# Two blocks of a transformer on one core: wider first accumulators, an unpaced GpSimd, and the pooling branch moved in among the attention's items

## The reference

```python
def adaln(cond, w, b):                       # w is 1024 x 9*1024
    m = jax.nn.silu(cond) @ w + b
    return m.reshape(m.shape[:-1] + (N_MOD, D_MODEL))

def ffn_sublayer(h, m, g, w13, w2, base):
    hn = modulate(rms_norm(h, g), m[:, :, base], m[:, :, base + 1])
    return h + 0.5 * m[:, :, base + 2] * swiglu_2(hn, w13, w2)

def multiscale_pool(u, pool_w, pool_scale):  # 4 groups of 128 channels, windows 2, 4, 8, 16
    ...
        mean = (jnp.take(cs, hi, axis=1) - jnp.take(cs, lo, axis=1)) / cnt
        outs.append((mean - xg).astype(u.dtype) @ pool_w[g])
    return jnp.concatenate(outs, axis=-1) * pool_scale

def even_mixer(hl, hc, w_in, w_out, rpb, pool_w, pool_scale, ctx_out):
    q, k, v, u = jnp.split(hl @ w_in, [NA_WIDTH, 2 * NA_WIDTH, 3 * NA_WIDTH], axis=-1)
    k_c, v_c = jnp.split(hc @ w_in[:, NA_WIDTH:3 * NA_WIDTH], 2, axis=-1)
    ...
    att = neighbourhood_attention(split_heads(q), split_heads(k), split_heads(v), k_c, v_c, rpb)
    pool = multiscale_pool(u, pool_w, pool_scale)
    y_lat = jnp.concatenate([att, pool], axis=-1) @ w_out
```

## Time and profile before

| | us |
|---|---|
| median of three timed runs | 2839.51 (2833.29 to 2842.50) |
| profiled execution | 2831.01 |
| its span | 2829.1 |
| mean granted TensorE clock | 0.943 |
| PE busy | 2634.2 |
| DVE busy | 1600.5 |
| ACT busy | 1173.0 |
| POOL busy | 1329.1 |

### The profile page before, as it was taken

How to read it: one execution, slowest core, us unless ns; L and a number is a source line. 1 busy time by engine, 2 the same in 40 slices (tenths; PEclk the granted TensorE clock), 3 DMA queues, 4 the chain that set the end, 5 groups by cost and what they waited for, 6 DMA issues and landing times.

```text
span 2829.1 us, 32645 instructions
## 1 busy us (share of the span) xinstructions
PE 2634.2 (93%) x11901; PEld 2141.4 (76%) x11901; DVE 1600.5 (57%) x1619; ACT 1173.0 (41%) x1354; POOL 1329.1 (47%) x689
## 2 busy tenths in 40 slices
PE   7997998899899899799989989998999999999998
PEld 6876766788688776678878777786678878878786
DVE  5664445656666634666666655544247666655544
ACT  4444344444443535444444433443134444353443
POOL 5994110399798211049959959700007535600000
PEclk9998999999999999999999989998579999998999
DMA  7663323567566422368767759843027757653553
GB/s 240 224 212 115 105 86 108 172 226 232 173 221 206 144 90 72 113 206 264 238 210 258 248 144 233 266 149 108 1 75 251 234 172 244 228 164 119 171 184 113
DMA packets 312483, 496.06 MB, mean 175 GB/s; under 512 B 14479, under 2 KB 221611, under 8 KB 312267
## 3 DMA queue, kind: packets, MB, share of 16 engines
q1 hardware_dynamic: 289306, 412.48, 44.8%
q0 software_dynamic: 22800, 81.35, 10.0%
q10 hardware_dynamic: 288, 1.05, 0.1%
HBM read 493.77 MB, written 1.05 MB: 175 GB/s over the span
## 4 chain that ended last, share of the span: by engine, by line
PE 60%; POOL 25%; DVE 5%; ACT 4%; DMA 3%; issue 2%; ACTq 0%; DVEq 0%; SPq 0%; POOLq 0%; PEldq 0%
PE ps L745 55%; POOL arena L688 11%; POOL arena L679 9%; POOL arena L689 3%; DMA raw<-in_ffn_w_dram 2%; PE ps L824 2%; POOL arena L663 2%; DVE wlo L433 2%; ACT whi L420 1%; PE ps L831 1%; PE ps L945 1%; PE ps L762 0%; PE ps L916 0%; ACT work L1212 0%; DVE HTlo L1415 0%
## 5 line engine op out<-in xcount | busy, mean ns | idle before, releaser
L433 DVE TENSOR_TENSOR wlo<-raw,whi 128x2048 fp32r<-128x2048 f32 (+5 forms) x405 | 1086.6, 2686 | 529.0 <-ACT whi L420 526.7
L745 PE MATMUL ps<-whi,HThi 128*128 128x512 f32 (+2 forms) x2360 | 957.5, 406 | 60.1 <-ACT arena L1203 20.2
L420 ACT ACTIVATE whi<-raw 128x2048 fp32r<-128x2048 f32 (+4 forms) x405 | 753.1, 1861 | 494.2 <-PE ps L745 412.2
L745 PE MATMUL ps<-wlo,HThi 128*128 128x512 f32 (+2 forms) x2360 | 932.3, 395 | 0.0
L745 PE MATMUL ps<-whi,HTlo 128*128 128x512 f32 (+2 forms) x2360 | 931.2, 395 | 0.0
L745 PEld LDWEIGHTS ps<-whi,HThi 128*128 128x128 f32 x2360 | 453.0, 192 | 162.1 <-issue 26.9
L688 POOL TENSOR_TENSOR arena<-arena 128x1024 f32<-128x1024 f32 (+1 forms) x184 | 541.0, 2940 | 10.8
L745 PEld LDWEIGHTS ps<-wlo,HThi 128*128 128x128 f32 x2360 | 452.0, 192 | 96.9
L745 PEld LDWEIGHTS ps<-whi,HTlo 128*128 128x128 f32 x2360 | 454.0, 192 | 85.7
L679 POOL TENSOR_TENSOR arena<-arena,cond 128x1024 f32<-128x1024 f32 x184 | 422.4, 2302 | 174.3 <-issue 85.5
L663 POOL DMA_DIRECT2D arena<-in_mod_w_dram x144 | 113.6, 789 | 470.6 <-DVEq L353 421.8
(11 more groups left out here) (196 smaller groups left out, 1756.9 us busy)
## 6 DMA issues: line engine op xcount, KB each, us to landing
raw<-in_ffn_w_dram SPq DMA_DIRECT2D x330, 512.0 KB, 4.7
raw<-in_w_ffn_gu_dram SPq DMA_DIRECT2D x176, 512.0 KB, 4.7
arena<-in_mod_w_dram POOLq DMA_DIRECT2D x144, 512.0 KB, 4.4
raw<-in_w_ffn_down_dram SPq DMA_DIRECT2D x88, 512.0 KB, 4.3
raw<-in_w_in_dram SPq DMA_DIRECT2D x40, 1024.0 KB, 5.1
raw<-in_even_w_in_dram SPq DMA_DIRECT2D x12, 1024.0 KB, 5.0
raw<-in_conv_w_in_dram SPq DMA_DIRECT2D x12, 1024.0 KB, 5.2
raw<-in_w_out_dram SPq DMA_DIRECT2D x8, 1024.0 KB, 5.0
```

Source lines behind the costliest of these rows:

```text
L420: i = nc.scalar.activation(whi[0:rows, r, a:b], raw[0:rows, r, a:b], ACT.Copy)
L433: i = nc.vector.tensor_tensor(wlo[0:rows, r, a:b], raw[0:rows, r, a:b], whi[0:rows, r, a:b].bitcast(F32), ALU.subtract)
L745: return nc.tensor.matmul(o, lhsT, rhs, start=first, stop=last)
```

## The change

- The accumulators of FFN 0 are 512 columns wide (`slots[0]`, twelve in `GT` and two in `C`), and POOL leaves out the last addition for them. PE adds both halves with two products per column instead of one.
- POOL's wait for PE's progress ahead of each piece is gone. For FFN 4 and later POOL waits, once per FFN and ahead of its DMAs, for the sums of earlier shares (`mods_summed`).
- The barriers of `near_turn` and `near` are gone; the turnings wait for the groups that they read (`group_read`), once ahead of them and once at the fifth chunk. The context's dense phase hands the copying of its last group on (`later=True`).
- In the pooling branch only the first group's average stays in `near_turn`, behind the turnings; the rest stands beside the items, a step at every other item. Averages use bank 6, maps bank 7; `pooled` and `pool_out` have places of their own.

```diff
-        slots = {**{f: [flat[:, MOD * i:MOD * (i + 1)] for i in range(24)] for f in (0, 1, 3)},
+        slots = {**{f: [flat[:, MOD * i:MOD * (i + 1)] for i in range(24)] for f in (1, 3)},
+                 0: [flat[:, 512 * i:512 * (i + 1)] for i in range(12)] + [C[:, 0, 512 * i:512 * (i + 1)] for i in range(2)],
...
-                phase("dense", after_norm=True,
+                phase("dense", after_norm=True, later=True,
...
-            if n and not phases[n]["kind"] in ("norm", "ffn", "final") and not phases[n].get("after_norm"):
+            if n and not phases[n]["kind"] in ("norm", "ffn", "final", "near_turn", "near") and not phases[n].get("after_norm"):
...
-        pool_out = [work[:, 512 + j * SEQ:512 + (j + 1) * SEQ] for j in range(2)]
+        pooled = [work[:, 3584 + j * SEQ:3584 + (j + 1) * SEQ] for j in range(2)]
+        pool_out = [flat[:, 5120 + j * SEQ:5120 + (j + 1) * SEQ] for j in range(2)]
...
-                    pool.wait_ge(s_used, ph["u0"] + 3 * (10 * i // len(part)) + 2)
...
-                        for n in (4 * MOD, 2 * MOD):
+                        n = 4 * MOD
+                        while n > acc.shape[-1]:
                             link(nc.gpsimd.tensor_tensor(q[:, 0:n], q[:, 0:n], q[:, n:2 * n], ALU.add))
-                        p = nc.gpsimd.tensor_tensor(acc, q[:, 0:MOD], q[:, MOD:2 * MOD], ALU.add)
+                            n //= 2
+                        p = nc.gpsimd.tensor_tensor(acc, q[:, 0:n], q[:, n:2 * n], ALU.add)
...
+                    if ph["f"] >= 4:
+                        pool.wait_ge(sem("mods_summed"), min(ph["f"] - 1, 5))
...
-            def turn(chunks, done, freed):
+            def turn(chunks, done, freed, at_4=lambda: None, behind=lambda: None):
...
+                    if m == 4:
+                        at_4()
...
+                behind()
...
-                    i = mm(o, acc, cc("ones"))
+                    for j, a in enumerate(acc):
+                        i = mm(o, a, cc("ones"), j == 0, j == len(acc) - 1)
...
-                    turn(near_chunks(), "heads_turned", ("heads_read_dve", "heads_read_act"))
-                    pe.wait_ge(sem("pool_in"), 32)
-                    for n_g in range(5):
...
-                    take("pool_split", 2)
+                    def average(g):
+                        for s in range(NB):
+                            i = mm(ps[:, 6, 0:SEQ], PJ[:, s, 1536 + g * P:1536 + (g + 1) * P], poolA[:, g, s, :], s == 0, s == 1)
+                        i.then_inc(sem("pooled"), 1)
+
+                    def first_average():
+                        pe.wait_ge(sem("pool_in"), 32)
+                        average(0)
+
+                    def pool_step(n):
+                        if n % 2 == 0 and n <= 6:
+                            g = n // 2
+                            take("pooled_copied")
+                            if g:
+                                take("pool_scaled")
+                            mm(ps[:, 7, 0:SEQ], poolW[:, g, :], pooled[g % 2]).then_inc(sem("pool_mapped"), 1)
+                            if g < 3:
+                                average(g + 1)
+
+                    take("group_read")
+                    turn(near_chunks(), "heads_turned", ("heads_read_dve", "heads_read_act"), lambda: take("group_read"), first_average)
...
-                    run_items(near_items())
+                    run_items(near_items(), (), pool_step)
```

More of the change, by code:

```diff
@@ L696, in bias_tiles @@
             def bias_tiles(h):
+                if h >= NA_H:
+                    return
                 rpb = t["na_rpb_2"]
-                for b in range(NB if h < NA_H else 0):
+                for b in range(NB):
                     for r in range(2):
@@ L782, in sums_of @@
                 pe.wait_ge(s_made, made)
-                accs = [acc[:, k * P:(k + 1) * P] for _, m, accs in parts for k in range(MOD // P) for acc in accs]
+                accs = [[acc[:, at:at + P] for at in range(k * P, acc.shape[-1], MOD)]
+                        for _, m, accs in parts for k in range(MOD // P) for acc in accs]
                 columns.extend((ps[:, bank, at:at + 1], acc) for at, acc in enumerate(accs))
@@ L810, in _, with run_items @@
             beside = Beside(part)
-            def run_items(items, places=()):
+            def run_items(items, places=(), between=beside.item):
                 N = len(items)
@@ L841, in run_items @@
                         i.then_inc(sem("item_pv"), 1)
-                    beside.item(n)
+                    between(n)
             def gate_rows(ph, half, bank):
@@ L1181, in turn_dst, with exps @@
                 return [(blocks[0].shape[-1], tile[0:blocks[0].shape[-1], m, :]) for m, blocks in enumerate(src)]
-            def exps(items):
+            def exps(items, between=lambda n: beside.item(n)):
                 for n, it in enumerate(items):
@@ L1345, in _, with pool_step @@
                 elif kind == "near":
-                    exps(near_items())
+                    def pool_step(n):
+                        if n % 2 and 3 <= n <= 9:
+                            take("pool_scaled")
+                            A(HThi[:, 4 + (n - 3) // 2, :], pool_out[(n - 3) // 2 % 2], ACT.Copy).then_inc(sem("pool_hi"), 1)
+                    exps(near_items(), pool_step)
                 elif kind == "near_turn":
                     copy_turned(near_chunks(), 1)
-                    for g in range(4):
-                        take("pool_scaled")
-                        A(HThi[:, 4 + g, :], pool_out[g % 2], ACT.Copy).then_inc(sem("pool_hi"), 1)
                 elif kind == "index":
@@ L1421, in _, with run_items @@
             pv_seen = [0]
-            def run_items(items, ys):
+            def run_items(items, ys, between=lambda n: beside.item(n)):
                 N = len(items)
@@ L1761, in _, with pool_step @@
                     copy_turned(near_chunks(), 0)
[L1762 to L1764 removed]
+                    take("pooled")
+                    V.tensor_copy(pooled[0], ps[:, 6, 0:SEQ]).then_inc(sem("pooled_copied"), 1)
+                elif kind == "near":
+                    out4 = work[:, 2048:3072].rearrange("p (b h d) -> p h b d", b=NB, d=HD)
+                    def pool_step(n):
+                        if n % 2 and n <= 5:
+                            g = (n + 1) // 2
                             take("pooled")
[L1766 to L1768 removed]
+                            V.tensor_copy(pooled[g % 2], ps[:, 6, 0:SEQ]).then_inc(sem("pooled_copied"), 1)
+                        if n % 2 and n <= 7:
+                            g = n // 2
                             take("pool_mapped")
[L1770 removed]
+                            V.tensor_scalar(pool_out[g % 2], ps[:, 7, 0:SEQ], vcol("pool_scale", g), None,
                                             ALU.mult).then_inc(sem("pool_scaled"), 1)
[L1772 to L1773 removed]
+                        if n % 2 == 0 and 4 <= n <= 10:
+                            g = n // 2 - 2
                             take("pool_hi")
```

23 lines of the change are left out of this document (1 added, 22 removed).

## The result

The changed kernel takes 2759.4 us (2754.0 to 2763.7, four runs), the kernel before 2840.3 beside it: ratio 0.9718, interval 0.9694 to 0.9743. Run again later, with the kernel before at 2834.1 beside it, it came to 0.9728 (0.9702 to 0.9754). So the gain is 77 to 81 us. The forecast was 2754. The profiled execution of the changed kernel took 2763.7 us, the longest of its four, where that of before was the shortest of its own; so the two traces differ by 67 us and the medians by 81.

What follows compares the result with a forecast made beforehand. The prediction took TensorE (PE), busy 93%, as the bound. Its terms sum to −85.5 us from the profiled 2831.0, giving 2745.5, and 8.5 added back gives 2754; own range 2742 to 2764 (62 in 100), wider range 2738 to 2793.

Steps and rivals of the forecast that it cites:

- The clock in the items: Attention's 16 items: at full clock, since pooling no longer stops PE, 109.5 us become 64.0, so −45.5.
- Rival 1: Attention: the items stay at the lower clock, so the kernel takes 2813 us; 12 in 100.
- The entry: Ahead of the attention's items: only the first average precedes the scores, so the first score comes 9.7 us earlier.
- FFN 0: End of FFN 0: wider accumulators end PE's wait for POOL, −16.5 us; more one-column products in mixer 0 cost +6.4.
- Rival 4: POOL is held by DVE, not its pace; FFN 1 and 4 keep their waits: 2767 us; 8 in 100.
- The second block's start: FFN 3 into the second block: POOL's earlier accumulator and context DMA shorten PE's wait, −3.4 us (0 to −5).
- FFN 4's end: End of FFN 4: POOL starts earlier, taking 7.3 us off PE's 12.80 us wait (−3 to −9).
- DVE against GpSimd: Starts of FFN 4 to 7: unpaced POOL slows DVE's split, +2 us (0 to +8).
- Rival 2: FFN 0 to 7: DVE becomes the bound when unpaced POOL meets its splits: 2844 to 2990 us; 2 in 100.
- FFN 5: In FFN 5 unpaced POOL runs ahead, its transfers starting earlier but denser: −3 us, between +6 and −6.
- rival 3: FFN 5: bias transfers bunch and starve the weights, losing 7 to 13 us: 2765 to 2770; 10 in 100.
- FFN 1: End of FFN 1: without its pace POOL starts earlier and shortens PE's wait, −6 us (−4 to −7).

Runs made afterwards that it cites:

- e3: Kernel before, pooling branch in its old place, PE's pauses there filled with four products of 512 fp32 columns nobody reads: 2783.8 us, ratio 0.9824.
- e5: Changed kernel with eleven more chained DVE copies behind item 7, when the pooling's products are done: 2780.7 us, ratio 0.9784 to the kernel before.
- e4: Changed kernel with seven more DVE copies that PE waits for ahead of the first item: 2770.1 us, ratio 0.9779 to the kernel before.
- e6: Kernel before with twelve products of 256 fp32 columns nobody reads, three beside each of items 0, 2, 4 and 6: 2801.2 us, ratio 0.9890.
- e1: Kernel before with only the attention's part of the change (barriers gone, pooling branch beside the items): 2774.0 us, ratio 0.9791.
- e9: Kernel before with only the 512-column accumulators in FFN 0, pace kept: 2830.6 us, ratio 0.9981.
- e2: Kernel before with only the modulation's part: 512-column accumulators in FFN 0 and no pace on GpSimd: 2816.8 us, ratio 0.9937.
- e8: The changed kernel run again unaltered, as base for later runs: 2759.8 us, ratio 0.9728 to the kernel before.
- e10: Kernel before with only GpSimd's pace gone and the new waits from FFN 4 on: 2818.9 us, ratio 0.9945.
- e7: Changed kernel with the attention's 32 bias DMAs issued behind FFN 5's modulation instead of among its pieces: 2740.7 us, ratio 0.9681 to the kernel before.
- e11: Changed kernel with GpSimd's pace back in FFN 5 alone: 2755.0 us, ratio 0.9719 to the kernel before.

## Why the prediction was right, step by step

**The clock in the items: right in cause, and shown.** Forecast 109.5 to 64.0, traced 65.2. e3 shows the cause without the move: fill PE's pauses, and the items run at 1.00. What the prediction had only as a worry, that slow items don't bring the clock back, is true for items alone (before, e5) and false for items with such products beside them (e4, e6). So the change protects twice: it takes the pause away, and after a pause ahead of the first item, as e4 shows, its products bring the clock back. Behind item 6, the last with pooling's products, that second protection ends. Rival 1 did not come in any of the changed kernel's eight executions, the longest of which took 2764.8 us.

**The entry.** Forecast −9.7. The traces show the first score 8.4 us nearer to the first turning, and the turning 1.5 us nearer to the dense phase: 9.9.

**Turning and gate behind the items.** −2.5 forecast, −0.4 measured. The step that failed is the clock: it no longer comes low out of the items, but it falls here at 2006, behind PE's waits of 1.15 and 2.25 us for DVE.

The terms outside the attention were read from one trace of each kernel. Other runs have the same code in these stretches, and their traces tell what is the change's and what the execution's. The numbers are us on PE. The old code stands in e1, e3 and e6 and, behind FFN 0, in e9; the changed code in e2, e4, e5 and e8, behind FFN 0 also in e10, and but for FFN 5 in e7 and e11:

| stretch | before | old code, others | changed | changed code, others |
|---|---|---|---|---|
| FFN 0's last turning to the mixer's first product | 27.3 | 27.3 | 14.5 | 14.5 to 15.4 |
| FFN 1's last turning to FFN 2's first product | 20.9 | 20.8 to 20.9 | 14.4 | 14.1 to 15.4 |
| FFN 3's last turning to FFN 4's first product | 25.8 | 23.6, 23.6, 23.6, 26.9 | 22.4 | 23.6 |
| FFN 4's first product to its second turning | 32.0 | 33.9 to 34.6 | 36.7 | 35.6 to 35.7 |
| FFN 4's last turning to FFN 5's first | 50.8 | 52.8 to 54.0 | 42.7 | 39.7 to 41.8 |
| FFN 5's first turning to its last | 180.0 | 178.2 to 183.6 | 183.0 | 183.7 to 185.2 |
| projection's first product to FFN 6's first turning | 42.6 | 42.6 to 43.0 | 45.0 | 45.1 to 46.0 |

**FFN 0.** −16.5 forecast; −12.9, and little more by the clock, which falls to 0.50 for 3.4 us at the mixer's start in the changed kernel too. The step that was mis-sized: GpSimd's early finish was taken as 23.5 us at unchanged durations; 10 went back into its own multiplications, and DVE's HTlo at the FFN's end takes 3.20 us beside it (1.29 in FFN 2), so PE has a new wait of 2.63 us. The columns cost 0.45 us in each of 14 pieces, 6.3, as forecast; before spent more of this stretch at the lower clock, and that hides 2 of them.

**FFN 1.** −6 forecast, −6.8 traced, and all traces agree: right. Rival 4, by which this wait and FFN 4's would stay, is out.

**The second block's start.** −3.4 forecast, −3.4 traced: luck. DVE's wait for the context's DMA, from which the term was read, is in the traces of before and e9 alone. e1, e3 and e6 have the old code too, and not the wait; they take 23.6 us there, as do the other runs of the changed code.

**FFN 4's end.** −7.3 forecast, −8.1 traced: near by luck, with the wait mis-sized. It was to shrink from 12.80 to about 5 us, and it is gone. GpSimd's last result comes 13.6 us earlier after the FFN's first product, 8.7 from its earlier start and 4.9 from running on without the pace. The trace of before was short here; the other pairs give 11 to 14.

The 3.3 us lost between FFN 2 and FFN 3 are clock: over the same 50 us of work its mean is 0.93 before (975 to 1025) and 0.87 in the changed kernel (959 to 1009), which is 3.0 us.

**DVE against GpSimd.** +2 forecast, too little. The pair of traces shows 4.8 us in FFN 4's first two steps (HTlo 3.73 us, PE's wait of 3.21 behind it). The other runs put it at 1 to 2 there, and all at 2 to 3 ahead of FFN 6; in e4, e5 and e8 FFN 7's first step takes 1.6 to 2.8 us more as well. The Trainium skill ("SBUF — State Buffer", two separate sides) says that the loser of the shared port blocks for the whole instruction; DVE's 1.47 to 3.73 us for the same pair agrees. GpSimd pays too: a multiplication takes 1.90 us where it meets none of those instructions, and 2.88 us on the mean in e9, where all meet one. Rival 2, a slower kernel by this, had the mechanism but not the size: the steady steps stayed 16.79.

**FFN 5: wrong in sign.** −3 forecast, +2.9 traced; the other runs give about +4, so rival 3 came in part. The row was there: a weight transfer of 8.5 us against 4.7. It was read as a risk of the change and not as a loss that before already had. e7 puts it at 13 us of before, and 16 to 18 of the changed kernel.

**Sum.** Attention: −57.7 forecast, −59 measured alone (e1). Modulation: −27.8 forecast, −18 (e2): FFN 5, DVE's price, FFN 0 and the second block's start fell short, and FFN 4's end gave more than forecast. The total, −85.5 forecast and −77 to −81 measured, was near because the large term was right.

## What to carry to other kernels

Where PE runs narrow fp32 products, look at the granted clock first and at PE's pauses ahead of the stretch second: two pauses, 1.00 and 1.69 us, cost 45 here, since the stretch kept the lower clock that it began with. Independent products beside such a stretch can be more than free: in e4 and e6 the clock came back with them. Before a row of one trace becomes a term, look whether a second execution has it. And when a helper engine is freed from its pace, recount its instructions at the durations they have beside DVE, and look at a stage whose DMAs already take twice their usual time before anything is sent there sooner.

## What was not expected of the hardware

- A kernel became 31 us faster by twelve products that nobody reads (e6), and 50 us faster by four (e3).
- PE at busy 5.00 of 5.00 stayed at 0.50 for 105 us with the items alone (before). With three products of 256 columns more at every other item it went back to 1.00 (e6, after 34 us; e4, after 7 us).
- Behind a pause of 1.13 us the clock was lost for the rest of the items (e5), by the times in three of four executions. A like pause in e3, and the pauses in mixer 0, show that it need not be.
- 32 DMAs of 64 KB among the weights and the modulation lengthened the landing of 512 KB transfers from 4.7 to 8.5 us, and an FFN by 13 us (before against e7).
- What stays open: why e6 needed 34 us to get the clock back and e4 only 7, why the same pauses are followed by a fall in some traces and not in others, and whether a denser arrangement of items 8 to 15 would guard them too.
